# Moving the causal mask of a stick-breaking attention kernel from TensorE matmuls to a VectorE add at the head of each slot

## What is computed

```python
h = rmsnorm(x, norm_g)
q, k, v, gate = split(h @ w_in, 4)
# per head, for query block q_pos (128 rows) and all keys:
mask = key_pos[None, :] < q_pos[:, None]
z = q @ k.T * 64 ** -0.5
log_beta = log_sigmoid(z)
log_1m = where(mask, log_beta - z, 0.0)
after = reverse_cumsum(log_1m) - log_1m
a = where(mask, exp(log_beta + after), 0.0)
o = a @ v
y = (o * silu(gate)) @ w_out
out = rmsnorm(x + y, final_g)
```

## Time and profile before

| what | value |
|---|---|
| median of 3 runs | 711.24 us (711.18 to 712.46) |
| the profiled execution's own time | 711.2 us |
| its span in the profile | 709.2 us |
| PE busy | 685.0 us, 97% |
| PE weight loads | 564.6 us, 80% |
| DVE busy | 479.6 us, 68% |
| ACT busy | 428.1 us, 60% |
| POOL busy | 293.4 us, 41% |
| PE share of the chain that ended last | 87% |

### The profile page before, as it was taken

The page is one execution under the profiler, slowest core; times in us unless marked ns, Lnnn a source line. Parts: engine busy times, 40 slices in busy tenths (PEclk is TensorE's granted clock), DMA queues, the critical chain, the costliest instruction groups (busy, mean ns, idle before and its releaser), DMA issues.

```text
span 709.2 us, 11132 instructions
## 1 busy us (share of the span) xinstructions
PE 685.0 (97%) x3554; PEld 564.6 (80%) x3554; DVE 479.6 (68%) x636; ACT 428.1 (60%) x795; POOL 293.4 (41%) x227
## 2 busy tenths in 40 slices
PE   5999999999999999999999999999999997999995
PEld 5787888888888888888888888888888775788884
DVE  5834757776677676766776677667776789745665
ACT  5615757676766666767666666666666575632422
POOL 2123444454444536454545353636363633414100
PEclk9999999999999999999999999999999999999999
DMA  7140410231014010410042014101411138623332
GB/s 283 44 105 29 104 31 16 66 113 34 28 50 129 30 32 28 137 44 15 30 119 74 15 31 118 59 30 30 119 59 30 60 116 262 247 89 89 120 139 98
DMA packets 28122, 57.64 MB, mean 81 GB/s; under 512 B 3376, under 2 KB 3376, under 8 KB 28080
## 3 DMA queue, kind: packets, MB, share of 16 engines
q1 hardware_dynamic: 25312, 51.13, 24.1%
q10 hardware_dynamic: 2736, 6.03, 2.2%
q0 software_dynamic: 32, 0.00, 0.0%
HBM read 37.23 MB, written 11.53 MB: 69 GB/s over the span
## 4 chain that ended last, share of the span: by engine, by line
PE 87%; DVE 6%; POOL 2%; ACT 2%; DMA 1%; issue 1%; ACTq 0%; POOLq 0%; DVEq 0%
PE proj_ps L487 44%; PE o_ps L636 9%; PE t_ps L648 9%; PE z_ps L583 9%; PE z_ps L562 8%; PE proj_ps L562 4%; DVE rest L1020 3%; PE o_ps L487 2%; POOL a_group L1120 1%; PE z_ps L585 1%; DMA a_group<-x 1%; PE t_ps L496 1%; POOL w_split L1096 1%; PE z_ps L507 0%; DVE gate L986 0%
## 5 line engine op out<-in xcount | busy, mean ns | idle before, releaser
L487 PE MATMUL proj_ps<-hT,w_split 128*128 128x512 f32 x1464 | 367.5, 399 | 2.0 <-DVE hT L893 1.5
L487 PEld LDWEIGHTS proj_ps<-hT,w_split 128*128 128x128 f32 x1464 | 266.4, 189 | 54.5 <-DVE hT L893 2.4
L1120 POOL TENSOR_TENSOR a_group<-a_group,rest 128x128 f32<-128x128 f32 (+7 forms) x128 | 159.4, 1248 | 301.2 <-DVE rest L1020 301.2
L1020 DVE TENSOR_TENSOR_SCAN rest<-rest 128x128 f32<-128x128 f32 (+7 forms) x128 | 213.4, 1668 | 20.8 <-ACT rest L813 19.2
L1004 DVE TENSOR_TENSOR aT<-t_ps,aT 128x512 fp32r<-128x512 f32 (+2 forms) x160 | 93.2, 607 | 41.4 <-ACT aT L798 39.8
L798 ACT ACTIVATE aT<-t_ps 128x512 fp32r<-128x512 f32 (+2 forms) x160 | 80.3, 532 | 65.0 <-PE t_ps L648 63.7
L1096 POOL TENSOR_TENSOR w_split<-w_raw,w_split 128x512 fp32r<-128x512 f32 x64 | 103.4, 1617 | 37.6 <-DVE w_split L855 37.6
L583 PE MATMUL z_ps<-arena 128*128 128x512 f32 (+2 forms) x384 | 98.3, 369 | 0.3 <-DVE arena L942 0.3
L942 DVE TENSOR_TENSOR arena<-stage,arena 64x512 fp32r<-64x512 f32 x64 | 43.9, 686 | 71.5 <-ACT arena L743 70.9
L813 ACT ACTIVATE rest<-z_ps 128x128 f32<-128x128 f32 (+7 forms) x128 | 83.8, 655 | 11.2 <-PE z_ps L585 10.9
L648 PE MATMUL t_ps<-ident,a_group 128*128 128x128 f32 x576 | 84.7, 275 | 2.1 <-POOL a_group L1120 1.8
(11 more groups left out here) (88 smaller groups left out, 488.8 us busy)
## 6 DMA issues: line engine op xcount, KB each, us to landing
w_raw<-w_in SPq DMA_DIRECT2D x64, 256.0 KB, 2.6
arena<-arena SPq DMA_DIRECT2D x32, 256.0 KB, 4.3
wo_raw<-w_out SPq DMA_DIRECT2D x16, 256.0 KB, 3.9
o_hi_scratch<-o_split SPq DMA_DIRECT2D x14, 256.0 KB, 2.1
o_lo_scratch<-o_split SPq DMA_DIRECT2D x14, 256.0 KB, 2.4
hT<-o_hi_scratch SPq DMA_DIRECT2D x14, 256.0 KB, 5.2
hT<-o_lo_scratch SPq DMA_DIRECT2D x14, 256.0 KB, 6.4
a_group<-x SPq DMA_DIRECT2D x14, 256.0 KB, 3.3
```

The costliest lines, as they stand in the source:

```text
L487: mm = nc.tensor.matmul(bank[:, :], w_split[:, ring, wl, b, :], hT[:, hl, b, half * HALF:(half + 1) * HALF], start=(b == 0 and n == 0), st ...
L1020: nc.vector.tensor_tensor_scan(span, span, span, 1.0, ALU.mult, ALU.bypass).then_inc(scan_done, 1)
L1120: nc.gpsimd.tensor_tensor(a, a, rest[:, s % 2, S + 1 - width:S + 1], ALU.mult).then_inc(a_ready, 1)
```

## The change

The mask is an fp32 table now, and VectorE adds it to the diagonal block of z in PSUM, as the first thing in its slot, behind z_ready. It raises a new semaphore, z_masked, for which ScalarE waits where it waited for z_ready. TensorE's mask matmul and both bf16 tables are gone, and z_ready is raised by the last matmul of the scores. In VectorE's slot the lower parts of the transposed weights (L1004) move from behind the lower parts of k and q, the gate and the sum of o to before them, right behind the mask. consts_ready counts to 3.

```diff
-        ident_16 = sb("ident_16", [P, P], BF16)
-        mask_16 = sb("mask_16", [P, P], BF16)
+        mask = sb("mask", [P, P])
...
+        z_masked = sem("z_masked")
...
-            pe.wait_ge(consts_ready, 4)
+            pe.wait_ge(consts_ready, 3)
...
                 for c in range(0, first + width, HALF):
                     c0, c1 = max(c, first), min(c + HALF, first + max(width, 2 * P))
-                    diagonal = c + HALF >= first + width
                     for swapped in (False, True):
                         mm = nc.tensor.matmul(z[:, c0:c1], q, k_of(par, hh, swapped)[:, c0 - first:c1 - first],
-                                              start=not swapped, stop=swapped and not diagonal)
-                mm = nc.tensor.matmul(z[:, first + width - P:first + width], ident_16[:, :], mask_16[:, :],
-                                      start=False, stop=True)
+                                              start=not swapped, stop=swapped)
                 mm.then_inc(z_ready, 1)
...
-                act.wait_ge(z_ready, SLOTS * p + s + 1)
+                act.wait_ge(z_masked, SLOTS * p + s + 1)
...
             def slot(p, par, s):
+                if not is_tail(p):
+                    i = s % 8
+                    diagonal = z_ps[s % 2][:, z_offset(i) + P * i:z_offset(i) + P * (i + 1)]
+                    if is_first(p) and s == 0:
+                        dve.wait_ge(consts_ready, 3)
+                    dve.wait_ge(z_ready, SLOTS * p + s + 1)
+                    nc.vector.tensor_tensor(diagonal, diagonal, mask[:, :], ALU.add).then_inc(z_masked, 1)
+                for t, av, _, grp, j in (units_at(p, s - 1) if s else av_at(p, 0)):
+                    rel = max(0, j - GQ * grp)
+                    dve.wait_ge(t_hi, t_base(p) + t + 1)
+                    if rel == GQ - 1:
+                        hi, lo = aT_pad[:, 0, P:2 * P], aT_pad[:, 1, P:2 * P]
+                    else:
+                        hi, lo = aT[:, av % 2, 0, rel * P:HALF], aT[:, av % 2, 1, rel * P:HALF]
+                    nc.vector.tensor_tensor(lo, t_ps[t % 2][:, rel * P:HALF], hi.bitcast(F32), ALU.subtract
+                                            ).then_inc(t_lo, 1)
                 evac = evac_at(p, s)
                 if evac:
                     kind, half, h = evac
...
                     nc.vector.tensor_tensor(oT[rows, cols], o_ps[rows, :], oT[rows, cols], ALU.add
                                             ).then_inc(o_summed, 1)
 
-                for t, av, _, grp, j in (units_at(p, s - 1) if s else av_at(p, 0)):
-                    rel = max(0, j - GQ * grp)
-                    dve.wait_ge(t_hi, t_base(p) + t + 1)
-                    if rel == GQ - 1:
-                        hi, lo = aT_pad[:, 0, P:2 * P], aT_pad[:, 1, P:2 * P]
-                    else:
-                        hi, lo = aT[:, av % 2, 0, rel * P:HALF], aT[:, av % 2, 1, rel * P:HALF]
-                    nc.vector.tensor_tensor(lo, t_ps[t % 2][:, rel * P:HALF], hi.bitcast(F32), ALU.subtract
-                                            ).then_inc(t_lo, 1)
                 if s in (2, 6) and not is_first(p):
...
-            for table in (ident, ident_16, mask_16):
+            for table in (ident, mask):
                 last = nc.gpsimd.memset(table[:, :], 0.0)
...
-            for table, keep, fill in ((ident, ALU.not_equal, 1.0), (ident_16, ALU.not_equal, 1.0),
-                                      (mask_16, ALU.is_gt, MASKED)):
+            for table, keep, fill in ((ident, ALU.not_equal, 1.0), (mask, ALU.is_gt, MASKED)):
```

More of the change, by code:

```diff
@@ L20 @@
 F32R = mybir.dt.float32r
-BF16 = mybir.dt.bfloat16
 P = 128
@@ L666, in _ @@
                 load_x_block(act, b)
-            act.wait_ge(consts_ready, 4)
+            act.wait_ge(consts_ready, 3)
             def root(cols, ready, count):
@@ L1016, in slot @@
                 span = rest[:, s % 2, S - 1:(S - 1 - width if width < S else None):-1]
-                if is_first(p) and s == 0:
-                    dve.wait_ge(consts_ready, 4)
                 dve.wait_ge(rest_ready, SLOTS * p + s + 1)
@@ L1116, in slot @@
                 if is_first(p) and s == 0:
-                    pool.wait_ge(consts_ready, 4)
+                    pool.wait_ge(consts_ready, 3)
                 pool.wait_ge(beta_ready, SLOTS * p + s + 1)
```

## The result

| what | before | after |
|---|---|---|
| median | 711.26 us (711.18 to 712.46, 4 runs) | 716.03 us (715.75 to 716.18, 4 runs) |
| ratio to before, 95% interval | | 1.0062 (1.0050 to 1.0074) |
| span of the profiled execution | 709.2 us | 714.1 us |
| PE busy | 97% | 95% |
| DVE busy | 68% | 73% |

A forecast was written before the change was run, and what follows sets the result against it. TensorE is full, but a VectorE-GpSimd line sharing the SBUF port runs right beside it and would bind. Pair 0 -0.6, pairs 1 to 6 +2.4, pair 7 -1.4: +0.4 on 711.2, so 711.6 us, range 703 to 717.5.

The forecast's parts named there:

- rival C: VectorE's queue of slots 4 and 12 runs past z of slots 5 and 13, so the mask waits: 718 us, 14%.
- Two sums of the rivals: TensorE stays the bound, 695.5 us, 7%; the forecast's own mechanism within its errors, 708.5 to 715 us, 60%.
- the line: VectorE's and GpSimd's port-sharing jobs, end to end before the transposes of slots 8 and 0; length of 15.4 us stays.
- step 3: New order in VectorE's slot: slot 13's scan about 1.5 us behind z (0.88 before); the line from slot 5 starts 0.48 later.
- Step 4: The line before the transposes of slots 8 and 0 only swaps jobs and ends later: +0.4 us a pair.
- Step 6: The ends: net -0.6 us in pair 0, its lower half -0.9 and upper +0.3; net -1.4 us in pair 7.
- such waits as what would show it wrong: TensorE waiting in slots 1 and 9 for VectorE's lower parts of the weights (L1004) or sum of o (L994).

The follow-up runs named there:

- e7: The kernel before with the mask matmul left out and nothing in its place, so the diagonal blocks are not masked; 702.82 us.
- e6: The changed kernel with the lower part of v of slot 8 moved ahead of that slot's scan; 713.91 us.
- e12: The changed kernel with the sum of o right behind the mask, ahead of the weights' lower parts, in slots 1, 5, 9 and 13; 714.47 us.
- e10: The changed kernel with the last pair's lower w_out parts of slots 5, 6 and 7 made one slot later, behind mask and weights' lower parts; 718.04 us.
- e13: e9 with the sum of o ahead of the weights' lower parts in slots 1, 5, 9 and 13; 703.25 us.
- e9: The changed kernel with GpSimd's second half of the next weights one slot later and the lower parts of v of slots 6 and 8 earlier; 705.24 us.
- e1: The changed kernel with the lower parts of the transposed weights put back behind the sum of o, the mask add staying first; 715.55 us.

## Why the forecast was right in its cause and short in its size

- **The number and its ranges.** 716.03 lies inside the wide range (703 to 717.5) but outside the forecast's own, 708.5 to 715, and the likeliest outcome by the chances was no change, not slower. The wide range reached so far only to cover rival C, whose mechanism is not what made the loss, so that the number falls into it is in part luck. On the profiled executions the sum was 4.5 us short: 1.8 in pairs 1 to 6, 2.2 in pair 7, 0.4 in pair 0. Two sums of the rivals were also not as stated: 711.2 - 16 is 695.2, not 695.5, and 711.6 with 2.6 on both sides is 709.0 to 714.2.
- **The cause held.** TensorE waits for multiply 7 and 15 as said, though for less than said (0.66 and 0.5 to 1.05 us, where 1.0 and 1.5 were forecast); the line kept its length (15.38 against 15.41); the mask of slot 5 starts 294.03 - 274.28 = 19.75 behind T0, at 19.79 by the working; L1108 runs behind scan 5; the scan of slot 13 starts 1.40 behind its mask (forecast 1.5 behind z); twelve projections behind scores take 2.72 to 2.76 in the chain. The add is 0.29, at 0.28 taken from the nearest row. e7 also bears out the price of a mask matmul: 1.2 us a pair shown (71.39 in place of 72.59 in pair 3) and some 0.5 of new waits in their place, of the 2.0 counted. The estimate by the Trainium skill (VectorE: DVE Perf Modes, The TRN2 errata) of 56 ns each would have been 7 us in all, under the 8.4 us that e7 measures.
- **The seams of step 3.** I took 0.08 off wherever VectorE starts one instruction before the end of the last. In slot 5 that fails at two of three seams: 294.24 + 0.68 to 294.96, and 294.96 + 0.69 to 295.68, a gap of 0.03 or so. In slot 13 they do overlap: 332.13 + 0.67 to 332.73. Two seams of 0.11 are 0.2 us, and the start of the line came 0.19 later than the 21.21 behind T0 (294.25 - 273.04) that I worked out. The sum of o in slots 1 and 5 is of the second head, which lies in the upper 64 partitions, and in slots 9 and 13 of the first. By the Trainium skill (VectorE: DVE Perf Modes, Two Vector instructions with no wait between them) an instruction whose operands start in another group of 32 partitions than the last one's is held until all earlier ones have finished. The trace agrees: of the 31 sums of o that follow without a wait, all 15 of slots 1 and 5 start 0.03 behind the end of the instruction before them, and all 16 of slots 9 and 13 start 0.08 ahead of it.
- **A wait I did not see, 0.36 a pair.** Step 4 asked what is late at T0 and T8 and stopped at the first wait. The second tile of the transposes at T8 waits for the v part behind scan 8. e6 takes it away for 2.1 us, and T8 to T0 is then 36.04, which is no loss at all. The scan of slot 13 does start 0.12 later behind T8 there (21.17 against 21.05 before), near the 0.1 to 0.2 that I had said, but the line behind it is shorter by most of that, so the 0.2 to 0.3 for T8 to T0 were not there.
- **Pair 0.** Step 6 counted 0.9 as won in the lower half; 0.2 came. TensorE's wait for ScalarE's copy in slot 2 grew from 0.33 to 1.12. Behind a table load of ScalarE (1.28 us at 60.40) the mask of slot 1 stands behind scan 0 (62.01 to 62.43, the mask at 62.35), and ScalarE's sigmoids wait for it, 62.66 in place of 61.72, with the copy in line behind them. This was read off the trace, not tried.
- **Pair 7.** This is the largest miss, -1.4 against +0.8. The clock did better than I said: in the profiled execution after it is 1.00 all through pair 7, so all of the 1.6 us came back, not a third. No wait foretells that, as the last point of this document shows: it was luck. The lower clock of before lay behind T8, so T8 to T0 without it was 30.46 - 1.6 = 28.9 by my estimate and is 30.85 now: new waits, less what the masks gave, took 2.0 there and 0.4 before T8. In step 3 the sum of o moved behind the mask and L1004 in slots 1, 5, 9 and 13, and I looked at its price on the line of slots 5 and 13 of a steady pair alone. With twelve matmuls of projection in a slot the rest is hidden. In slots 0 to 9 of the last pair there are six (1.54 us at 573.34), not twelve as my account of the kernel has it, and there it is not hidden: TensorE waits 0.99, 0.41 and 0.99 us for that sum. The prediction had named such waits as what would show it wrong, but not the pair in which they could come. e12 shows 2.0 us of it, in its lowest execution.
- **Rival C's mechanism** was real but not what bound: the mask stood in line for 1.4 us in slot 6 of the last pair, and e10 shows that freeing it buys nothing there, as multiply 5 has the port.

## What to carry to other kernels

When two engines feed each other through a shared resource, lay their jobs end to end and compare that length with the bounding engine's time before taking work from it: here 2.0 us a pair less on TensorE could bring 1.2 at best (e7), and two thirds of a microsecond more in front of the line turned it into a loss. To gain, shorten that line: moving one 1.3 us product of each half pair out of it was worth 10 us on the changed kernel, and with the v parts and the sum of o earlier as well the changed kernel beats the old one by 8.0 us (e13). And count the cost of each moved step once in the steady pair and once at each end, where less work hides it.

## What was not expected of the hardware

- Who asks first decides who waits, by hundredths. L1108 takes 1.30 us when it asks ahead of scan 5 and 2.80 when it asks 0.05 us behind; the other side pays too (scan 5: 1.76 or 2.35). In slot 7 of the same pair L1096 starts at 305.49 and takes 1.28, and scan 7 starts at 305.50 and takes 3.42; before, the scan was first, with 2.41, and L1096 took 3.27. The Trainium skill (SBUF — State Buffer, SBUF: two separate sides) says that the first to start has the pair of ports for its whole instruction, and the rows shown here agree. A scan of 128 columns, 0.62 us by itself in e6, took 1.89 where it asked behind multiply 7.
- The mask add reads and writes PSUM at 267 to 300 ns for 128 columns, and runs inside GpSimd's instructions without being stretched.
- Two instructions of VectorE that follow each other overlap by 0.08 us or leave 0.03 between them; at the sums of o a fixed slot has always the same of the two.
- What TensorE is granted in the last pair could not be told from its waits. In the kernel before the clock is 0.50 (the lower of the two levels, 1.2 GHz) for 3.2 us behind one wait of 3.9 us. In the kernel after it is 1.00 (2.4 GHz) all through that pair, with waits of 0.88, 1.08, 0.80 and 0.59 us in slots 6 to 8. In e9 the same four waits are 0.90, 1.08, 0.80 and 0.59, and behind them the clock is 0.50 from 586 to 588 us and 0.69 from 588 to 590. e1 has 0.79 and 0.70. The cause stays open. That some executions get the lower clock may be why e1's six runs lie between 714.3 and 718.75; only the slowest of them has a trace.
